# Rotary partner rows by small on-chip copies from ScalarE's queue instead of a matmul with a swap matrix

## What is computed

```python
A_ROT = A_HEAD_DIM // 4          # 16 of 64 channels
C_ROT = C_HEAD_DIM // 4          # 16 of 64 channels

def apply_rope(x, cos, sin):
    r = cos.shape[-1]            # 8
    ...
    x1, x2 = xf[..., :r], xf[..., r:]
    rot = jnp.concatenate([x1 * c - x2 * s, x2 * c + x1 * s], axis=-1)
    return jnp.concatenate([rot, x[..., 2 * r:]], axis=-1)

def diff_attention(h, w_qkv, ...):          # layers 0 and 3
    qkv = h @ w_qkv                         # 1024 q, 1024 k, 1024 v channels
    q = apply_rope(q, cos, sin); k = apply_rope(k, cos, sin)
    ...
def dilated_attention(h, w_qkv, ...):       # layer 2: three groups of q, k, v
    q = apply_rope(qkv[:, :, :, 0], cos, sin); k = apply_rope(qkv[:, :, :, 1], cos, sin)
    ...
```

## Time and profile before

| | |
|---|---|
| median of 3 runs | 3060.56 us |
| the profiled execution | 3069.05 us |
| its span in the profile | 3067.3 us |
| TensorE matmul busy | 91% of the span |
| VectorE busy | 51% |
| ScalarE busy | 32% |
| DMA queue of SyncE | 56.0% of 16 engines |
| granted TensorE clock, mean | 0.94 |

### The profile page before, as it was taken

One profiled execution on the slowest core, in us unless ns is written; L12 is line 12 of the kernel. 1 busy time (PEld: TensorE's weight loads), 2 busy tenths in 40 slices (PEclk: granted clock), 3 DMA queues, 4 the chain that ended last, 5 costly groups with the idle time before them and its releaser, 6 DMA issues.

```text
span 3067.3 us, 51379 instructions
## 1 busy us (share of the span) xinstructions
PE 2802.8 (91%) x20226; PEld 2246.8 (73%) x20226; DVE 1549.1 (51%) x2785; ACT 993.4 (32%) x1522; POOL 0.2 (0%) x4
## 2 busy tenths in 40 slices
PE   6887999999999999876998899999987799995998
PEld 6776655556555555765998559999975599983998
DVE  4654233233332333556766436676655566666665
ACT  3332112112212121334434324443333343433433
POOL 0000000000000000000000000000000000000000
PEclk9987999999999999987998779999989999995999
DMA  6342899999999999631552305544430045540453
GB/s 232 129 143 112 347 422 422 422 422 422 422 422 422 422 422 422 238 110 41 179 181 99 108 15 178 180 171 171 165 123 1 1 151 179 178 165 0 152 179 110
DMA packets 93043, 665.53 MB, mean 217 GB/s; under 512 B 10336, under 2 KB 10464, under 8 KB 12672
## 3 DMA queue, kind: packets, MB, share of 16 engines
q1 hardware_dynamic: 92928, 663.90, 56.0%
HBM read 662.81 MB, written 1.05 MB: 216 GB/s over the span
## 4 chain that ended last, share of the span: by engine, by line
PE 79%; DVE 10%; DMA 6%; ACT 2%; SPq 2%; issue 1%; DVEq 0%; ACTq 0%
PE bank L265 14%; PE bank L267 14%; PE bank L266 14%; PE bank L1420 12%; DMA big<-wdn 5%; PE bank L1437 5%; PE bank L691 5%; PE bank L1408 3%; PE bank L705 2%; DVE small L756 2%; PE bank L1468 2%; SPq L1358 2%; PE bank L721 1%; ACT w_hi L247 1%; PE bank L885 1%
## 5 line engine op out<-in xcount | busy, mean ns | idle before, releaser
L255 DVE TENSOR_TENSOR w_lo<-ring,w_hi 128x2048 fp32r<-128x2048 f32 (+2 forms) x253 | 558.5, 2208 | 332.4 <-ACT w_hi L247 332.1
L265 PE MATMUL bank<-ht_hi,w_hi 128*128 128x256 f32 x2260 | 656.5, 290 | 8.0 <-DVE w_lo L255 6.0
L247 ACT ACTIVATE w_hi<-ring 128x2048 fp32r<-128x2048 f32 (+2 forms) x253 | 466.4, 1844 | 549.5 <-PE bank L267 522.5
L266 PE MATMUL bank<-ht_lo,w_hi 128*128 128x256 f32 x2260 | 641.5, 284 | 0.0
L267 PE MATMUL bank<-ht_hi,w_lo 128*128 128x256 f32 x2260 | 641.5, 284 | 0.0
L265 PEld LDWEIGHTS bank<-ht_hi,w_hi 128*128 128x128 f32 x2260 | 435.6, 193 | 17.9 <-DVE w_lo L255 8.3
L266 PEld LDWEIGHTS bank<-ht_lo,w_hi 128*128 128x128 f32 x2260 | 435.9, 193 | 7.5 <-issue 7.4
L267 PEld LDWEIGHTS bank<-ht_hi,w_lo 128*128 128x128 f32 x2260 | 435.7, 193 | 0.0
L1420 PE MATMUL bank<-ring,big 128*64 128x256 f32 x2048 | 236.9, 384 | 0.9 <-ACT big L1485 0.9
L1420 PE MATMUL bank<-moe_w,big 128*64 128x256 f32 x2048 | 235.1, 382 | 0.0
L1615 DVE TENSOR_SCALAR big<-bank,big 128x64 f32<-128x64 f32 x256 | 60.9, 279 | 337.4 <-PE bank L1427 337.4
(11 more groups left out here) (245 smaller groups left out, 4129.2 us busy)
## 6 DMA issues: line engine op xcount, KB each, us to landing
ring<-post SPq DMA_DIRECT2D x211, 1024.0 KB, 4.8
ring<-wgu SPq DMA_DIRECT2D x128, 1024.0 KB, 18.5
moe_w<-wgu SPq DMA_DIRECT2D x128, 1024.0 KB, 20.4
moe_w<-wdn SPq DMA_DIRECT2D x96, 1024.0 KB, 22.1
big<-wdn SPq DMA_DIRECT2D x32, 1024.0 KB, 23.4
ring<-pre SPq DMA_DIRECT2D x28, 1024.0 KB, 4.9
ring<-post SPq DMA_DIRECT2D x6, 384.0 KB, 3.1
ring<-post SPq DMA_DIRECT2D x8, 256.0 KB, 2.9
```

Of the source, the lines that this page charges most:

```text
L247: act.activation(w_hi[:, u % SR, 0:w], ring[:, u % R, 0:w], ACT.Copy).then_inc(ph.hi, 1)
L255: dve.tensor_tensor(w_lo[:, u % SR, 0:w], ring[:, u % R, 0:w], f32(w_hi[:, u % SR, 0:w]), ALU.subtract).then_inc(ph.lo, 1)
L265: pe.matmul(out, wh, xh, start=start and k == k0, stop=False, **kw)
L266: pe.matmul(out, wh, xl, start=False, stop=False, **kw)
```

## The change

For the two stages that used `rot_ac`, the rotation matmul is left out. After its copy to `raw`, ScalarE issues four copies from SBUF to SBUF of 8 partitions x 512 columns (16 KB each), two for each of the two heads in the tile, which lay the rows i + 8 at i and the rows i at i + 8 in a new buffer `swapped` (columns 512 to 1536 of `prob`, two halves used in turn). The minus sign of the rotation moves into the sin table (`first=-1.0`). The other 96 rows of `swapped` are never copied; the sin there is 0, and VectorE sets the whole buffer to 0 once at each stage's start. VectorE's `m2` reads `swapped` instead of the PSUM bank and waits for the four copies. The table of constants loses `rot_ac` (128 of its 2819 columns).

```diff
@@ const_table
-    put("rot_ac", rotation(64, 0, 8))
-    put("cs_ac", rope_table(64, 0, 8))
+    put("cs_ac", rope_table(64, 0, 8, -1.0))
@@ rope_table(head, at, r, first=1.0)
-    s[at:at + r], s[at + r:at + 2 * r] = np.sin(ang).T, np.sin(ang).T
+    s[at:at + r], s[at + r:at + 2 * r] = first * np.sin(ang).T, np.sin(ang).T
@@ program
+        s_swap, s_blank = [sem(f"rope_swapped{a}") for a in range(2)], sem("rope_rows_blank")
...
+        swapped = flat[:, 512:1536].rearrange("p (a n) -> p a n", a=2)
@@ rope_stage
+            w0 = swap_count[0]
+            tables0 = table_count[0]
+            if hand is not None:
+                table_count[0] += 1
+            if rot is None:
+                swap_count[0] += per_r * times
@@ rot_one
+                if R_ is None:
+                    return
@@ body_act, behind the copy to raw
+                    if R_ is None:
+                        if hand is not None and isinstance(i, int) and l == 0:
+                            act.wait_ge(s_blank, tables0 + 1)
+                        act.wait_ge(s_raw, r + 1 + i * per_r)
+                        for at in (0, 64):
+                            act.dma_start(swapped[at:at + 8, r % 2, :], raw[at + 8:at + 16, r % 2, :]).then_inc(s_swap[r % 2], 16)
+                            act.dma_start(swapped[at + 8:at + 16, r % 2, :], raw[at:at + 8, r % 2, :]).then_inc(s_swap[r % 2], 16)
@@ body_dve
                     hand.reduce(dve)
+                    dve.wait_ge(s_hss, hand.j + 1)
+                    dve.memset(swapped, 0.0).then_inc(s_blank, 1)
...
-                    dve.wait_ge(s_rot, r + 1 + i * per_r)
-                    dve.tensor_tensor(m2, blocks(bank[1 + r % 2][:, :]), sin2, ALU.mult).then_inc(s_link, 1)
+                    if R_ is None:
+                        dve.wait_ge(s_swap[r % 2], 64 * ((w0 + index(l)) // 2 + 1) + i * (32 * per_r))
+                    else:
+                        dve.wait_ge(s_rot, r - w0 + 1)
+                    turned_rows = swapped[:, r % 2, :] if R_ is None else bank[1 + r % 2][:, :]
+                    dve.tensor_tensor(m2, blocks(turned_rows), sin2, ALU.mult).then_inc(s_link, 1)
@@ the calls for layers 0, 3 and 2
-                t = rope_stage(f"a_qkv{l}", ..., hts, none, c("rot_ac"), c("cs_ac"), hand=h_a)
+                t = rope_stage(f"a_qkv{l}", ..., hts, none, None, c("cs_ac"), hand=h_a)
-                t = rope_stage("c_qkv", ..., hts, none, c("rot_ac"), c("cs_ac"), times=3, step=8, hand=h_a)
+                t = rope_stage("c_qkv", ..., hts, none, None, c("cs_ac"), times=3, step=8, hand=h_a)
```

More of the change, by code:

```diff
@@ L89, in rotation, with rope_table @@
     return np.kron(np.eye(P // head), m)
-def rope_table(head, at, r):
+def rope_table(head, at, r, first=1.0):
     pos = np.arange(S, dtype=np.float32)
@@ L840, in program @@
         table_count = [0]
+        swap_count = [0]
         def rope_stage(name, ph, dram, u0, spec, src, src_ready, rot, tabs, kc=KB, times=1, step=0, hand=None):
@@ L923, in body_dve @@
                         dve.tensor_tensor(blocks(scaled), blocks(tabs), rows2, ALU.mult).then_inc(s_tab, 1)
-                        dve.wait_ge(s_tab, 1 + table_count[0])
-                        table_count[0] += 1
+                        dve.wait_ge(s_tab, tables0 + 1)
                     if not spec[l][1]:
@@ L1662, in program @@
                 spec = [("T", True, 2 * i) for i in range(8)] + [("N", False, (16, i)) for i in range(4)]
-                t = rope_stage(f"a_qkv{l}", POST_PH, post, POST["a_qkv", l], [(*x_, 0) for x_ in spec], hts, none, c("rot_ac"), c("cs_ac"), hand=h_a)
+                t = rope_stage(f"a_qkv{l}", POST_PH, post, POST["a_qkv", l], [(*x_, 0) for x_ in spec], hts, none, None, c("cs_ac"), hand=h_a)
                 va = area(16, 8).rearrange("p (t n) -> p t n", t=NT)
@@ L1737, in program @@
                 spec = [("T", True, 2 * i, 0) for i in range(4)] + [("T", True, 24 + 2 * i, 0) for i in range(4)] + [("N", False, (48, i), 0) for i in range(4)]
-                t = rope_stage("c_qkv", POST_PH, post, POST["c_qkv", l], spec, hts, none, c("rot_ac"), c("cs_ac"), times=3, step=8, hand=h_a)
+                t = rope_stage("c_qkv", POST_PH, post, POST["c_qkv", l], spec, hts, none, None, c("cs_ac"), times=3, step=8, hand=h_a)
                 vc = [area(48 + 8 * j, 8).rearrange("p (t n) -> p t n", t=NT) for j in range(3)]
```

## The result

The change makes the kernel slower: 3080.02 us (median of 8 runs, 3068.96 to 3083.75) against 3064.65 us for the kernel before in its 8 runs (3058.93 to 3072.38). The ratio is 1.0045, with a 95% interval of 1.0027 to 1.0064. The forecast was 3032 us, 3025 to 3050, and faster; both the sign and the range were wrong. The profiled execution took 3079.19 us, its span 3077.4 (before: 3069.05 and 3067.3).

What follows compares the result with a forecast made beforehand. The prediction took TensorE to bound the rotated tiles: -34.2 us for the removed matmuls and +5.8 us for stage-start stalls gave -28.4 us, from the median 3060.56 to 3032 us, range 3025 to 3050.

Steps and rivals of the forecast that it cites:

- The matmul's 0.855 us a tile: On TensorE, removing the rotation matmul saves 0.855 us in each of 40 tiles, -34.2 us in all.
- The stall at the start, 3 x 1.94 us: At tile 4 of three stages TensorE waits for VectorE's rest of unit 4, losing 1.94 us each, +5.8 us.
- The memset, about 0.9 us and hidden: VectorE's zeroing of the buffer at each stage's start takes about 0.9 us, covered by other waits, costing nothing.
- With 0.33 the fourth issue begins at T + 3.44: On ScalarE, at SyncE's 0.33 us an issue, the last copy goes out 3.44 us after the split's start T.
- The bound of 0.8 above: Upper limit for one copy issue, 0.8 us, at which four would fill ScalarE's 5.76 us period.
- The last, which counts, goes out when the load is done: Argument against copies waiting: the previous tile's load lands at T + 3.3, the copies go out T + 2.45 to 3.44.
- the 4.0 that the sum allowed: The copies' landing may take 4.0 us after the last issue before TensorE loses anything.
- The landing as one number: Time from the last copy's issue to its landing, taken as 2.6 us from the router's 128 KB load.
- the rival: Copies wait behind weight loads at VectorE's m2: landing 7.4 us or 8.6, total 3071 or 3087 us, chance 0.09.
- The period, (13.25 + landing) / 3: Tile period for late landings: 5.76 us at a landing of 4.0, the old 6.61 at 6.6.
- The rule: DMA engines finish a packet of 9 to 17 descriptors before switching queues, so a copy could wait for most of a load.
- ScalarE as the bound: Rival: issues of about 1.0 us each fill ScalarE's period, so no gain, 3060 us, chance 0.04.

Runs made afterwards that it cites:

- e1_nocopy: Changed kernel without the four copies per tile and without VectorE's wait for them (rotated rows incomplete): 3043.65 us, ratio 0.9919 to the kernel before.
- e4_sp_issue: Changed kernel with the four copies issued by SyncE on the weight loads' queue, ahead of its next load: 3043.01 us, ratio 0.9914 to the kernel before.
- e6_order: e4_sp_issue with VectorE's rest of unit 4 moved ahead of the rotation of tile 1 at stage starts: 3035.41 us, ratio 0.9905 to the kernel before.
- e3_gated: Changed kernel, all four copies, SyncE issuing a weight load only once the copies that would meet it have landed: 3045.33 us, ratio 0.9929 to before.
- e7_shift: Changed kernel with q and k channels reordered and ScalarE moving partner rows from PSUM itself, no DMA copies: 3043.21 us, ratio 0.9919 to before.
- e9_three: Changed kernel with the last of the four copies left out (partner terms incomplete): 3050.11 us, ratio 0.9938 to the kernel before.

## Why the prediction was wrong

- **The matmul's 0.855 us a tile: right.** Steady tiles are 5.76 us apart in every version whose copies land in time.
- **The stall at the start, 3 x 1.94 us: right** (1.95 in e1_nocopy, 1.92 in e4_sp_issue). The two terms together, -28.4, show in e1_nocopy: of the -22.6 in the table its attention parts have +5.1 (94.33 against 89.69 us behind layer 0, 94.36 against 93.19 behind layer 3, 189.95 against 190.68 behind layer 2), and the end of tile 1 in layer 2 has +0.6 (8.89 against 8.26 us), which leaves -28.3. Why the attention behind a stage takes up to 4.6 us more at times stays open.
- **The memset, about 0.9 us and hidden: right.** It takes 0.91. The one distance of e1_nocopy that is longer than before where no rotation is involved, the 8.89, isn't its work: e6_order has the memset and 8.27 there, and before, layer 3 has 8.93 without it. The difference goes with a slow stretch of the clock.
- **"With 0.33 the fourth issue begins at T + 3.44": the step that failed.** The row taken was that of loads from HBM. An issue of a copy within SBUF takes 0.63 us and comes every 0.66, so the fourth goes out at T + 4.41. The bound of 0.8 above held; the value between the ends did not.
- **"The last, which counts, goes out when the load is done": false by that.** The sentence before it had the load at T + 4.3 (measured 4.26). The copy slid from 0.9 us ahead of the next load to 0.15 behind it, and with it went the landing: 4.88 us, over the 4.0 that the sum allowed and over the 3.1 that were left of it with the issue at T + 4.41. I had set the copy against the load of the tile before and never asked how near it came to the one ahead of it, though both numbers stood there.
- **The landing as one number: false.** It depends on the loads: 2.0 us with none near, 4.9 to 5.4 when issued within 0.15 us of one, 2.9 to 4.7 when issued 2.2 to 3.0 behind one. The line drawn down to 16 KB, 2.1, was the better estimate of the quiet one than the 2.6 I took. The late one is less than the 7.4 of the rival, since the copy lands with the load and not a full time of its own after it.
- **The period, (13.25 + landing) / 3: right as a form.** With 4.41 for 3.44 and 4.88 for the landing, three periods are 4.41 + 4.88 + 1.45 + 2.34 + 6.02 = 19.10 us; layer 0 has 5.76 + 5.75 + 7.58 = 19.09. Only every third tile's landing counts: VectorE works off one late unit, TensorE waits once, and two tiles run at full pace.
- **The clock: no term for it at all.** At 19.10 us for three tiles the period is 6.37, still under the 6.61 of before. The 15 new waits are 29.5 us of idle time, and each lengthens its distance by 0.26 more than that (1.98 us of idle time stand in a distance of 7.99, 2.23 over 5.76; in e1_nocopy 1.69 in one of 7.71). That makes 33.4 us, which would have eaten the 34.2 gained and no more. Against 5.76 a tile, the distances behind tile 1 lost 46.8 us; the 13.4 that the waits don't cover are nine slow stretches of 1.5 us. So the waits alone would have made this change about nothing; the granted clock made it slower. That split is worked out from one trace, and no run removes the one and keeps the other.
- **The rule:** that a copy issued behind a load comes only with it is what the Trainium skill, DMA: Bandwidth & Descriptors, section "Queues, rings and completion order", would have one expect (an engine finishes a packet of descriptors before it turns to another queue). The trace agrees: the copy issued beside the load has its records at the end of the load's, and m2 starts 4.88 us after the issue against 2.0 with no load near. I gave this rival 0.09, on the argument that failed above. That its price, 3071 to 3087 us, holds the measured 3080 is luck: it put 7.4 us or more on every tile and nothing on the clock; measured are 4.9 to 5.4 on mostly every third tile, and slow stretches.

ScalarE as the bound, the other way in which dear issues could hurt, had little part: e3_gated and e7_shift put about the same load on it and gain 0.7 and 0.8%.

## What to carry to other kernels

A small transfer that something waits for has more than one price when large loads run beside it: here 2.0 us if it is issued 0.4 us or more ahead of a 1 MB load with none running, and 4.9 or more if issued together with one. Lay the issue times of both on one axis with their margins, price an issue by a row of its own kind of transfer, and where the margin is under a microsecond put the small one on the loads' own queue ahead of them (here worth 1.3%). When work is taken off the engine that bounds, look at the stage starts which that work covered (an order of two steps that was worth nothing before took 1.6 us off each stage start once the matmuls were gone), and count a wait of about 2 us on TensorE as the wait plus a possible slow stretch behind it.

## What the runs showed of the hardware that was not expected

- Issuing a copy within SBUF takes 0.61 to 0.63 us in the median on ScalarE's and on SyncE's queue, with 8 partitions and 16 KB or with 16 and 32 KB; a 1 MB load from HBM takes 0.33 on SyncE's. Why the small one is dearer stays open.
- A copy issued between 0.15 us ahead of a 1 MB load on another queue and 0.15 behind it lands 4.9 to 5.4 us later; one issued 0.42 us or more ahead of it, with no other load running, 2.0 (the kernel after and e9_three).
- TensorE's granted clock fell to the lower level for about 3 us after 9 of the 15 new waits of the kernel after, and the length of the wait doesn't tell which: of three waits of 1.84 us those that end at 1329.72 and 2240.51 us have no slow stretch behind them, and the one that ends at 2259.88 has. The stage starts of e1_nocopy and e4_sp_issue, with waits of 1.67 to 1.69, have none. What decides it wasn't tried.
